# Low weight parts of odd units on GpSimd: a two-layer encoder trunk with a three-term float32 matmul

## What is computed

```python
for i in range(DEPTH):
    if i % N_MIXERS == 0:
        x = x + mlstm_mixer(x, *mix_params[i])
    else:
        x = x + diff_attn_mixer(x, positions, *mix_params[i], lambda_init=lambda_init)
    x = x + peer_ffn(x, *ffn_params[i])
```

## Time and profile before

| | us |
|---|---|
| median of 3 runs (lowest, highest) | 1957.85 (1954.58, 1960.06) |
| the profiled execution | 1955.85 |
| its span, first to last instruction | 1954.0 |
| TensorE matmuls busy | 1917.6 (98%) |
| TensorE weight loads busy | 1713.3 (88%) |
| VectorE busy | 1423.9 (73%) |
| ScalarE busy | 914.6 (47%) |
| GpSimd busy | 17.4 (1%) |
| DMA engines' busy share, HBM rate | 51%, 166 GB/s |
| share of the chain that ended last: TensorE, VectorE | 93%, 4% |

### The profile page before, as it was taken

One profiled execution on the slowest core, in us unless ns is written; L12 is line 12 of the kernel. 1 busy time (PEld: TensorE's weight loads), 2 busy tenths in 40 slices (PEclk: granted clock), 3 DMA queues, 4 the chain that ended last, 5 costly groups with the idle time before them and its releaser, 6 DMA issues.

```text
span 1954.0 us, 37852 instructions
## 1 busy us (share of the span) xinstructions
PE 1917.6 (98%) x13760; PEld 1713.3 (88%) x13762; DVE 1423.9 (73%) x2491; ACT 914.6 (47%) x1263; POOL 17.4 (1%) x20
## 2 busy tenths in 40 slices
PE   8999999999999999999998899999999999999998
PEld 7778999999998888888876589999999988888887
DVE  5455599977777888655578657998777778886555
ACT  5454444544444444444465744445443444444444
POOL 0000000000000000000000000100000000000000
PEclk9999999999999999999999999999999999999999
DMA  6504456555455555555554154565454555555554
GB/s 220 173 1 162 151 172 193 175 170 171 163 162 165 175 175 173 183 193 193 193 172 150 45 161 151 172 193 183 162 166 164 164 164 176 176 174 191 193 192 164
DMA packets 89482, 326.09 MB, mean 167 GB/s; under 512 B 10064, under 2 KB 10192, under 8 KB 89040
## 3 DMA queue, kind: packets, MB, share of 16 engines
q1 hardware_dynamic: 88848, 323.00, 50.9%
q10 hardware_dynamic: 576, 2.33, 0.3%
HBM read 324.24 MB, written 1.05 MB: 166 GB/s over the span
## 4 chain that ended last, share of the span: by engine, by line
PE 93%; DVE 4%; ACT 2%; issue 1%; DMA 1%; SPq 0%; DVEq 0%; ACTq 0%
PE ps L1223 15%; PE ps L1224 15%; PE ps L1225 15%; PE ps L1432 12%; PE ps L1434 12%; PE ps L1433 12%; PE ps L1381 3%; PE ps L1247 2%; PE ps L1248 2%; PE ps L1249 2%; DVE wl L702 1%; PE ps L1320 1%; PE ps L1363 1%; PE ps L1194 1%; DMA raw<-stream 1%
## 5 line engine op out<-in xcount | busy, mean ns | idle before, releaser
L702 DVE TENSOR_TENSOR wl<-raw,wh 128x1024 fp32r<-128x1024 f32 x612 | 737.2, 1227 | 188.8 <-ACT wh L417 180.1
L417 ACT ACTIVATE wh<-raw 128x1024 fp32r<-128x1024 f32 x612 | 644.8, 1055 | 448.8 <-PE ps L1225 209.4
L1223 PE MATMUL ps<-hTh,wh 128*128 128x256 f32 x2376 | 679.0, 286 | 2.8 <-DVE hTl L712 2.8
L1224 PE MATMUL ps<-hTl,wh 128*128 128x256 f32 x2376 | 672.7, 283 | 0.0
L1225 PE MATMUL ps<-hTh,wl 128*128 128x256 f32 x2376 | 672.6, 283 | 0.0
L1223 PEld LDWEIGHTS ps<-hTh,wh 128*128 128x128 f32 x2376 | 456.4, 192 | 3.6 <-issue 1.8
L1224 PEld LDWEIGHTS ps<-hTl,wh 128*128 128x128 f32 x2376 | 456.5, 192 | 0.0
L1225 PEld LDWEIGHTS ps<-hTh,wl 128*128 128x128 f32 x2376 | 456.2, 192 | 0.0
L1432 PE MATMUL ps<-wh,hTh 128*128 128x512 f32 x1024 | 405.1, 396 | 0.0
L1434 PE MATMUL ps<-wh,hTl 128*128 128x512 f32 x1024 | 399.5, 390 | 0.0
L1433 PE MATMUL ps<-wl,hTh 128*128 128x512 f32 x1024 | 398.4, 389 | 0.0
(11 more groups left out here) (201 smaller groups left out, 1217.4 us busy)
## 6 DMA issues: line engine op xcount, KB each, us to landing
raw<-stream SPq DMA_DIRECT2D x612, 512.0 KB, 3.4
big<-keys ACTq DMA_DIRECT2D x2, 1024.0 KB, 7.8
x<-x_in SPq DMA_DIRECT2D x1, 1024.0 KB, 5.7
out<-x SPq DMA_DIRECT2D x4, 256.0 KB, 2.2
sm<-small ACTq DMA_DIRECT2D x1, 228.5 KB, 5.9
pos_i<-positions ACTq DMA_DIRECT2D x1, 1.0 KB, 6.8
```

The lines of the kernel that those rows point to most:

```text
L417: act.activation(wh[:, r, :], raw[:, r, :], ACT.Copy).then_inc(high_ready, 1)
L702: dve.tensor_tensor(wl[:, r, :], raw[:, r, :], wh[:, r, :].bitcast(F32), ALU.subtract).then_inc(split_ready, 1)
L1223: pe.matmul(out, w_h[:, kd, :], hTh[:, kd, :], start=(kd == 0), stop=False)
L1224: pe.matmul(out, w_h[:, kd, :], hTl[:, kd, :], start=False, stop=False)
```

## The change

A low part is made by VectorE if its unit is even and by GpSimd if it is odd. The semaphore `split_ready` becomes two, `low_even` (from VectorE) and `low_odd` (from GpSimd), and SyncE's and TensorE's waits ask for the one of their unit, at half the count. GpSimd's program makes its low parts in the order of the units; between them come its four additions, at units 16 and 28 of each up projection (CAND_AT). VectorE's calls of `low` for odd units return without an instruction.

```diff
+        CAND_AT = 16, 28
+        def made_low(unit):
+            return low_odd if unit % 2 else low_even
...
-                    sp.wait_ge(split_ready, RING * turn + (r + 1 - RING))
+                    sp.wait_ge(made_low(r), RING // 2 * turn + (r // 2 + 1 - RING // 2))
...
+            def low(unit, turn):
+                pool.wait_ge(high_ready, offset(turn, RING, unit + 1))
+                r = unit % RING
+                pool.tensor_tensor(wl[:, r, :], raw[:, r, :], wh[:, r, :].bitcast(F32), ALU.subtract
+                                   ).then_inc(low_odd, 1)
+            def lows(a, b):
+                turns = (a + RING - 1) // RING, b // RING
+                for u in range(a, RING * turns[0]):
+                    if u % 2:
+                        low(u, None)
+                with pool.Fori(turns[0], turns[1]) as turn:
+                    for r in range(1, RING, 2):
+                        low(r, turn)
+                for u in range(RING * turns[1], b):
+                    if u % 2:
+                        low(u, None)
+            at = 0
             for l in range(2):
                 for t in range(NT):
+                    to = unit_of[f"u{l}"] + CAND_AT[t]
+                    lows(at, to)
+                    at = to
                     pool.wait_ge(val_ready, NT * l + t + 1)
                     pool.wait_ge(hi_bank_free, HI * l + 4)
...
+            lows(at, UNITS)
...
             def low(unit, turn):
+                if unit % 2:
+                    return
                 dve.wait_ge(high_ready, offset(turn, TURN, unit + 1))
                 r = unit % RING
                 dve.tensor_tensor(wl[:, r, :], raw[:, r, :], wh[:, r, :].bitcast(F32), ALU.subtract
-                                  ).then_inc(split_ready, 1)
+                                  ).then_inc(low_even, 1)
...
             def split(unit, turn=None):
-                pe.wait_ge(split_ready, offset(turn, TURN, unit + 1))
+                pe.wait_ge(made_low(unit), offset(turn, TURN // 2, unit // 2 + 1 if unit % 2 == 0 else (unit + 1) // 2))
```

More of the change, by code:

```diff
@@ L209, in program @@
         high_ready = sem("high_ready")
-        split_ready = sem("split_ready")
+        low_even = sem("low_even")
+        low_odd = sem("low_odd")
         used = sem("used")
```

## The result

With the change the kernel takes 1964.06 us (median of 7; 1963.54 to 1968.91), before 1957.85 us (median of 7). The ratio is 1.0041, with a 95% interval of 1.0031 to 1.0052; the quotient of the two medians, 1.0032, lies in it. So the kernel is 6 to 8 us slower, just past what I had called "about the same" (0.3%). The forecast was 1959.4 us, with 1953 to 1963 as its own range: the result lies above that, and inside the whole range of 1951 to 1980. The profiled execution took 1964.0 us with a span of 1962.2 us, 8.2 us more than the profiled one of before (the medians are 6.2 us apart).

A forecast was written before the change was run, and what follows sets the result against it. TensorE was taken as the bound, VectorE only in qkv. Terms -0.5 - 0.4 + 0.4 + 2 = +1.5 us on the profiled 1955.85 gave 1957.4, as a median 1959.4; own range 1953 to 1963, whole range 1951 to 1980.

The forecast's parts named there:

- GpSimd's time: One low part on GpSimd: 2.1 us, with ends of 1.85 and 3.70 from the row of its 128x2048 addition.
- The exclusion: VectorE instructions with two SBUF inputs and GpSimd reading SBUF exclude one another for a whole instruction.
- Up projections and the down projections' second half: GpSimd's low parts fit between VectorE's two-input instructions in these stages: cost nothing.
- Down projections' first half: The tightest stage, 6.05 us a pair of units: cost nothing with GpSimd's low part at 2.1 to 2.7 us.
- p: GpSimd's time for one low part; in the down projections' first half lasting loss was to begin at 2.7 us.
- (a): Rival: GpSimd's instruction is long, the shared port bounds the down projections' first half; about 1990 to 2020 us, chance 0.14.
- qkv: qkv stage: 16.8 us blocked, less 9.6 saved and 3.6 present idle, +3.6; ends -1 and +5, taken +2 us.
- the tie: qkv: odd high part ready at 1018.07, VectorE's next two-input instruction at 1018.17, again in each block of four units.
- Entry and seams: Start -0.5 us, ends of the two output projections -0.4, first GpSimd low parts of the qkv stage +0.4.
- (b): Rival: all qkv ties go against VectorE (+5), or late val_ready delays odd low parts (+2 to +3); about 1965, chance 0.11.
- (d): Rival: VectorE's instructions stretch by as much as it gave away; time of forecast or (b), chance inside the forecast's 0.68.
- (c): Rival: VectorE's freed 367 us matter where the waits do not show; 1952.8 us at best, chance 0.07 beyond 5.9 us.

The follow-up runs named there:

- e4: The changed kernel with one more GpSimd subtraction of 128x256 into a spare buffer ahead of each of its low parts: 2002.48 us, ratio to before 1.0238.
- e6: The changed kernel with one more GpSimd subtraction of 128x512 into a spare buffer ahead of each of its low parts: 2036.56 us in one run.
- e8: The changed kernel, but in units 305 to 331 GpSimd makes only 305, 309 and so on, VectorE the other odd ones: 1962.52 us, ratio to before 1.0032.
- e5: The changed kernel, but in units 305 to 331 GpSimd only writes zeros into odd low parts and reads nothing: 1955.0 us in one run.
- e2: GpSimd makes only the odd low parts of units 305 to 331 (qkv), VectorE all others as in the kernel before: 1964.34 us, ratio to before 1.0042.
- e1: The changed kernel, but VectorE makes the odd low parts of units 305 to 331 (qkv) as before: 1955.78 us, ratio to before 0.9996.

## Why the prediction was right or wrong

**What bounds the kernel.** Right. TensorE is at 170 of 170 and 174 of 174 us in the long stages, before and after, and the freed 330 us of VectorE bought nothing there. The ceiling for a gain (1952.8 us) held in the changed kernel and in all eight experiments: the lowest median is 1955.67 us, the one single run at the low end 1955.0.

**GpSimd's time (2.1 us).** Too low: 2.40 us undisturbed. I started from half the row of the 2048-column addition (1.85 us) and guessed a fixed share, but that row is of another kind of operand: both its inputs are broadcast. The pieces of e4 and e6 give the line for plain inputs: 0.74 us for 256 columns, 1.29 for 512, 2.40 for 1024, so 2.2 ns a column and 0.2 us fixed. By that line 2048 columns would take 4.6 us and not 3.70; that the broadcast inputs make the difference is likely, but no run isolates it. By the estimate from the Trainium skill, "GPSIMD Engine Reference", section 3.1 (about 2.25 us), the page was nearer to the measured 2.40 than my half row or my 2.1.

**The exclusion.** Right, and shown anew in both directions (3.44 for 1.22 us in the trace; 3.46 for 2.40 in e8). The Trainium skill, "SBUF — State Buffer", section "Who interferes with whom", says that a two-input VectorE instruction contends with a GpSimd instruction that reads, not with one that only writes; by e5 the trace agrees (1.22 us beside a fill).

**Up projections and the down projections' second half.** Right in the time: the FFN of each layer grew by 0.4 us of 765. For the first half of the up projections the reason was incomplete. I had only the low parts down as instructions with two SBUF inputs; the four multiplications of the slot comparisons in each layer went from 1.22 to 3.43 us, and a cast, with one input, from 0.43 to 2.51. That is 11 us of VectorE's time per layer, and it cost nothing because VectorE had the room. "One input" is not enough to be safe from GpSimd: MAX8 was undisturbed in the earlier trace rows, this cast was not.

**Down projections' first half.** The forecast of no loss was right, the margin was wrong. I had lasting loss begin at p = 2.7 us, because weigh would slide under GpSimd's time. In the changed kernel GpSimd starts during hots_i, and hots_j pays (start us, us; compare):

```profile
701.45 0.68 DVE L1053 TENSOR_TENSOR hTl<-big,hTh 128x512 fp32r<-128x512 f32 x1
702.05 0.68 DVE L1015 SCALAR_TENSOR_TENSOR big<-ps,big 128x512 f32 x1
702.65 0.41 DVE L994 TENSOR_TENSOR same_j<-iota_h,slot_d 128x512 f16<-128x512 f16 x1
702.98 0.68 DVE L999 TENSOR_TENSOR hots_i<-iota_h,slot_d 128x1024 f16<-128x1024 f16 x1
703.58 2.88 DVE L1004 TENSOR_TENSOR hots_j<-same_j,gate_d 128x1024 f16<-128x1024 f16 x1
706.39 1.21 DVE L736 TENSOR_TENSOR wl<-raw,wh 128x1024 fp32r<-128x1024 f32 x1
707.52 0.68 DVE L1053 TENSOR_TENSOR hTl<-big,hTh 128x512 fp32r<-128x512 f32 x1
```

A pair is 6.07 us where TensorE needs 6.05: the stage stands on the edge. e4 added 0.7 us to the port and lost 15 us a layer at p of about 3.1, where my rule (0.4 over, times 32, less 4.4) gave 8.4. The rival (a) was the right mechanism, but it begins sooner than at p = 2.7: at 2.40 VectorE has nothing left. The kernel missed it by a hair, and that the term came out as forecast is in part luck.

**qkv.** The step that failed. The mechanism, the place and the tie were named in advance; the size was +2, with an upper end of +5, and it was +9.0. The sum was 16.8 - 9.6 - 3.6, and of the +3.6 that it gives I took about half. The 16.8 held: from 1014 us on, eight stretches on VectorE come to 17.0 us. The 3.6 us of "present idle time" are what was wrong in it. From 1014 us to the end of the stage, 2.8 us of VectorE's idle time before were waits for ScalarE's squares after the evacuation of a bank, and in the changed kernel they are 3.7 us ([0.70 <-ACT] in three of its four blocks). Idle time that is part of a chain is not room for something else. Without that term the sum is +7 to +8 us.

On TensorE's side the 9.0 us are these: its waits for low parts grew from 0.5 to 7.2 us, 1.1 of it at the entry, and of the other 2.3 us, 1.4 are a clock that fell once. After the stall of 2.43 us the granted clock was 0.70 in the next five microseconds:

```profile
1041.00:1046.00 5.00, 5.00 (x16) 4.00 (x17) 4.24 (x6) 3.29 (x5) 1.13 (x1) 0.70 0.63 217
```

The matmuls in it:

```profile
1041.51 0.63 PE L1282 MATMUL ps<-wl,hTh 128*128 128x512 f32 x1
1041.94 0.63 PE L1283 MATMUL ps<-wh,hTl 128*128 128x512 f32 x1
1042.37 0.63 PE L1281 MATMUL ps<-wh,hTh 128*128 128x512 f32 x1
```

Matmuls start 0.43 us apart there and 0.23 at the full clock of 2.4 GHz: half the clock, for about seven of them, 1.4 us. e2 had a stall of 2.44 us at the same place with a granted clock of 1.00 behind it:

```profile
1042.00:1047.00 5.00, 4.76 (x21) 3.94 (x22) 4.23 (x7) 3.63 (x5) 0.81 (x1) 1.00 0.59 210
```

Its stage was only 0.4 us shorter, because its next wait for VectorE was 2.43 us where the changed kernel's was 0.99. So the lower clock comes and goes, and nearly all of the time that it took was time in which TensorE would have waited. The cause of the loss is VectorE's block, not the clock.

**Entry and seams.** Entry of qkv: +0.4 forecast, 1.1 to 1.2 us measured. Start and seams: -0.9 together; e1, with all of them and without the qkv part, is at 0.9996 (0.9987 to 1.0005), so they are smaller than a measurement can tell.

**The signs.** Of the signs in the prediction, the pair is 6.07 us where more than 6.05 was to prove it wrong, GpSimd's operation 2.40 us where 1.9 to 2.3 was expected, and the qkv stage 9.0 us longer where 1 to 5 was expected. TensorE waited 1.1 us for GpSimd's low parts, under the 5 of the text.

**The rivals.** (b) had the mechanism (all clashes of the qkv stage against VectorE) at 1965 with 0.11, and the result is 1964.06. But its 1965 was +5 in the qkv stage and +2 to +3 for odd low parts queued behind val_ready. The first was +9.0 and the second didn't occur, since TensorE never waited there; that the total fits is luck. The result lies in the whole range because that range was drawn to take in (b), and not by the forecast's sum. (d), stretched instructions, is true as an observation: VectorE's busy time fell from 1423.9 to 1263.9 us, 160 us for 306 low parts given away. (c) is out.

## What to carry to other kernels

Before moving work between VectorE and GpSimd, take for each stage VectorE's work in one turn as it will be after the move and add GpSimd's reading instructions to it, nearly in full. In this kernel that gives the measured turns: 3.87 + 2.2 = 6.07 us for a pair, 9.3 + 2 x 2.2 = 13.7 us for a block of the qkv stage. If the sum passes the turn of the engine that sets the pace (here 6.05 and 10.9 us), the stage is lost once the lead is used up, and in e8 it didn't help that VectorE came first. Find the one stage where the engine to be relieved sets the pace, and reckon there per block with the chain as it is, idle waits included. Where nothing waits for the relieved engine, as outside this kernel's qkv stage (75 of 1954 us), the runs show nothing to win, only something to lose.

## What was not expected of the hardware

- GpSimd's two-input operation costs 2.2 ns a column and 0.2 us on plain operands (0.74, 1.29, 2.40 us for 256, 512, 1024 columns), and its addition of broadcast ones took 3.70 us for 2048, less than the 4.6 us of that line.
- A VectorE cast of 128x512 from uint32 to f16, with one SBUF input, took 2.51 us beside GpSimd's reading and 0.43 without it. MAX8 and FIND_INDEX8, with one input too, did not grow.
- A GpSimd instruction that waits for the port gets it before VectorE's next two-input instruction, though that stands right behind (e8: GpSimd's record begins at 1018.61, VectorE's instruction ended about 1019.8, the next one was stopped; the same in the next two blocks).
- In none of the traces read here did the VectorE instruction with one input in PSUM, TensorE's output memory, and one in SBUF (weigh) grow: it took 0.67 to 0.70 us in all of them, also where it lay beside GpSimd's reading, as most of them did in e6.
